# All columns of w_down as split products, a one-operation one-hot comparison, and table columns read by TensorE

## What is computed

```python
h = rmsnorm(x, g_pre_ffn[l]) * (1.0 + sc2) + sh2
gates = route(h, w_router, router_bias)        # 64 experts, 8 chosen for each token
g = jnp.einsum('sd,edf->sef', hs, w_gate)      # (1024 -> 256) for each expert
u = jnp.einsum('sd,edf->sef', hs, w_up)        # (1024 -> 256)
act = jax.nn.silu(g) * u * gs[:, :, None]
routed = jnp.einsum('sef,efd->sd', act, w_down)  # (256 -> 1024)
shared = (jax.nn.silu(h @ ws_gate) * (h @ ws_up)) @ ws_down
x = x + ga2 * rmsnorm(routed + shared, g_post_ffn[l])
```

## Time and profile before

| what | value |
|---|---|
| runs | 1063.95, 1064.50, 1066.36 us |
| the profiled execution | 1069.23 us |
| its span, first to last instruction | 1067.2 us |
| PE busy | 1020.3 us, 96% of the span |
| DVE busy | 872.1 us, 82% |
| ACT busy | 645.2 us, 60% |
| POOL busy | 295.4 us, 28% |
| L1366, the float32 half of down | 129.4 us busy in 272 records |
| L1372, the split half of down | 81.3 us busy in 136 records of the first form |
| L1845, `wdlo` | 82.7 us busy, 1216 ns each, x68 |
| L943, `wdhi` | 72.2 us busy, 1061 ns each, x68 |
| L1801, the one-hot comparisons | 61.2 us busy, 280 ns each, x284 |

### The profile page before, as it was taken

One profiled execution on the slowest core, in us unless ns is written; L12 is line 12 of the kernel. 1 busy time (PEld: TensorE's weight loads), 2 busy tenths in 40 slices (PEclk: granted clock), 3 DMA queues, 4 the chain that ended last, 5 costly groups with the idle time before them and its releaser, 6 DMA issues.

```text
span 1067.2 us, 15239 instructions
## 1 busy us (share of the span) xinstructions
PE 1020.3 (96%) x4652; PEld 742.9 (70%) x4652; DVE 872.1 (82%) x1416; ACT 645.2 (60%) x743; POOL 295.4 (28%) x224
## 2 busy tenths in 40 slices
PE   4999999899998999999999999999999999999976
PEld 0687776567754777777777777777777777777732
DVE  1669877734768899999999889999989999999867
ACT  5334135733343678777777767777767777777511
POOL 1242231630302433223323213323313323332200
PEclk9899999989999999999999999999999999999997
DMA  9667752212254799999999999999999999999993
GB/s 338 263 223 280 267 179 97 69 30 90 99 217 146 284 376 373 364 381 379 393 386 381 360 367 359 377 376 385 369 364 345 364 343 328 353 354 362 361 413 152
DMA packets 71080, 318.67 MB, mean 299 GB/s; under 512 B 17232, under 2 KB 17744, under 8 KB 44560
## 3 DMA queue, kind: packets, MB, share of 16 engines
q1 hardware_dynamic: 36816, 200.30, 49.7%
q10 hardware_dynamic: 11616, 72.66, 17.9%
q0 software_dynamic: 22624, 45.40, 11.4%
HBM read 317.25 MB, written 39.85 MB: 335 GB/s over the span
## 4 chain that ended last, share of the span: by engine, by line
PE 80%; DVE 9%; DMA 7%; ACT 2%; issue 1%; ACTq 0%; SPq 0%; POOL 0%; DVEq 0%; POOLq 0%
PE ps L1348 11%; PE ps L1350 11%; PE ps L1349 11%; PE ps L1366 10%; PE ps L1033 8%; PE ps L1372 8%; PE ps L1123 6%; DMA hg<-h_rows,idxg 3%; PE ps L1225 2%; DMA yr<-y_rows 2%; PE ps L1285 2%; PE ps L1049 2%; PE ps L1305 1%; PE ps L1207 1%; DVE acc L1504 1%
## 5 line engine op out<-in xcount | busy, mean ns | idle before, releaser
L1821 DVE TENSOR_TENSOR wlo<-raw,whi 128x2048 fp32r<-128x2048 f32 x136 | 305.2, 2285 | 0.0
L891 ACT ACTIVATE whi<-raw 128x2048 fp32r<-128x2048 f32 x136 | 261.4, 1923 | 0.0
L1348 PE MATMUL ps<-whi,hthi 128*128 128x512 f32 x544 | 223.9, 412 | 0.0
L1350 PE MATMUL ps<-whi,htlo 128*128 128x512 f32 x544 | 213.5, 393 | 0.0
L1349 PE MATMUL ps<-wlo,hthi 128*128 128x512 f32 x544 | 212.7, 391 | 0.0
L661 POOL DMA_INDIRECT y_rows<-ysb,idxs x68 | 69.1, 1016 | 447.8 <-DVE idxg L1816 387.2
L934 ACT ACTIVATE ysb<-ps 128x1024 f32<-128x1024 f32 x68 | 69.8, 1026 | 176.1 <-PE ps L1372 176.1
L653 POOL DMA_INDIRECT hg<-h_rows,idxg x70 | 135.9, 1942 | 71.9 <-DVE idxg L1816 51.6
L1366 PE MATMUL ps<-rawd,actt 128*128 128x512 f32 x272 | 129.4, 598 | 1.9 <-ACT actt L927 1.9
L1350 PEld LDWEIGHTS ps<-whi,htlo 128*128 128x128 f32 x544 | 102.1, 188 | 22.3
L1349 PEld LDWEIGHTS ps<-wlo,hthi 128*128 128x128 f32 x544 | 102.6, 189 | 17.7
(11 more groups left out here) (273 smaller groups left out, 1608.7 us busy)
## 6 DMA issues: line engine op xcount, KB each, us to landing
raw<-in_w_gate_dram SPq DMA_DIRECT2D x68, 1024.0 KB
raw<-in_w_up_dram SPq DMA_DIRECT2D x68, 1024.0 KB
rawd<-in_w_down_dram ACTq DMA_DIRECT2D x66, 1024.0 KB, 10.1
ada<-in_w_ada_dram SPq DMA_DIRECT2D x24, 1024.0 KB, 7.8
yr<-y_rows SPq DMA_DIRECT2D x6, 2048.0 KB, 19.1
wraw<-in_w_in_dram POOLq DMA_DIRECT2D x8, 1024.0 KB, 5.6
woraw<-in_w_out_dram SPq DMA_DIRECT2D x16, 256.0 KB, 2.7
yr<-y_rows SPq DMA_DIRECT2D x8, 512.0 KB, 10.1
```

The source lines that it names most:

```text
L891: A(whi[:, s, m_, :], raw[:, s, m_, :], ACT.Copy).then_inc(hi_ok, 1)
L1348: mm(out_, hthi[s][:, k, :], hi, start=(k == 0), stop=False)
L1350: ins = mm(out_, htlo[s][:, k, :], hi, start=False, stop=(k == KD - 1))
L1821: V.tensor_tensor(wlo[s][:, m_, :], raw[:, s, m_, :], whi[:, s, m_, :].bitcast(F32), ALU.subtract).then_inc(lo_dve, 1)
```

## The change

In `down`, the columns 512 to 1023 of `w_down` are also made of three split products, so PE has 12 fp32r products for each block. `down_high` and `down_low` work on both halves, in two operations each, and `wdhi[hf]` now belongs to a half, where it belonged to a slot. `down` waits for `actl` first, then for each half of `wdlo`. `actt` stays, as an operand of `actl`. `onehot` becomes one `tensor_tensor` of 4x128 elements, with both inputs broadcast, and without the copy to `vcur`; `indices` reads `vtab` at the block's number. PE therefore waits for `fill_ok` ahead of its loop, and its loop is cut in the same places as that of DVE. In the tail, `y_out(last, 0)` goes ahead of `down_high(last, 1)`.

```diff
--- before.py
+++ after.py
@@ -940,7 +940,8 @@
 
             def down_high(i, s):
                 ac.wait_ge(wd_in[s], i * 16 + 16)
-                A(wdhi[s][:, :, :], rawd[:, s, :, 0:DC], ACT.Copy).then_inc(wdhi_ok, 1)
+                for hf in range(2):
+                    A(wdhi[hf][:, :, :], rawd[:, s, :, hf * DC:(hf + 1) * DC], ACT.Copy).then_inc(wdhi_ok, 1)
 
             def step_act(i, s, late, e=None):
 
@@ -1012,8 +1013,8 @@
             down_high(last, 0)
             act_rows(last, 0)
             silu(last, 1)
+            y_out(last, 0)
             down_high(last, 1)
-            y_out(last, 0)
             act_rows(last, 1)
             y_out(last, 1)
 
@@ -1322,11 +1323,14 @@
                 ins.then_inc(count_mm, 1)
 
 
-            def indices(i, s):
+            def indices(i, s, shift=0):
 
                 pe.wait_ge(onehot_ok, num(i, s) + 1)
+                b = num(i, s) + shift
                 for t in range(TT):
-                    ins = mm(ps[:, 7 * BANK:7 * BANK + VC], s_onehot[:, t, :], vcur[:, t, :],
+                    src = vtab[:, t, b, :] if isinstance(b, int) else \
+                        vtab[:, t, bass.ds(b, 1), :].rearrange("p b v -> p (b v)")
+                    ins = mm(ps[:, 7 * BANK:7 * BANK + VC], s_onehot[:, t, :], src,
                              start=(t == 0), stop=(t == TT - 1))
                 ins.then_inc(idx_mm, 1)
 
@@ -1358,23 +1362,21 @@
                 ins.then_inc(at_tr, 1)
 
             def down(i, s):
-                pe.wait_ge(wd_in[s], i * 16 + 16)
-                pe.wait_ge(actt_ok, num(i, s) + 1)
+                pe.wait_ge(actl_ok, num(i, s) + 1)
                 if not (isinstance(i, int) and num(i, s) == 0):
                     pe.wait_ge(y_ok, num(i, s))
-                for k in range(KF):
-                    mm(bank(5), actt[:, k, :], rawd[:, s, k, DC:D], start=(k == 0), stop=(k == KF - 1))
-                pe.wait_ge(wdlo_ok, num(i, s) + 1)
-                pe.wait_ge(actl_ok, num(i, s) + 1)
-                for k in range(KF):
-                    for j, (a_, w) in enumerate(((acth, wdhi[s][:, k, :]), (acth, wdlo[:, s, k, 0:DC]),
-                                                 (actl, wdhi[s][:, k, :]))):
-                        ins = mm(bank(4), a_[:, k, :], w, start=(k == 0 and j == 0), stop=(k == KF - 1 and j == 2))
+                for hf in range(2):
+                    pe.wait_ge(wdlo_ok, num(i, s) * 2 + (hf + 1))
+                    for k in range(KF):
+                        hi, lo = wdhi[hf][:, k, :], wdlo[:, s, k, hf * DC:(hf + 1) * DC]
+                        mm(bank(4 + hf), acth[:, k, :], hi, start=(k == 0), stop=False)
+                        mm(bank(4 + hf), acth[:, k, :], lo, start=False, stop=False)
+                        ins = mm(bank(4 + hf), actl[:, k, :], hi, start=False, stop=(k == KF - 1))
                 ins.then_inc(dn_mm, 1)
 
-            def block_pe(i, s):
+            def block_pe(i, s, shift=0):
                 rows_in(*after(i, s, 1))
-                indices(*after(i, s, 3))
+                indices(*after(i, s, 3), shift)
                 gate_up(i, s, 0, 3)
                 acts_tr(*after(i, s, -1))
                 gate_up(i, s, 3, KD)
@@ -1426,14 +1428,16 @@
             mm(ps[:, OV + 128:OV + 128 + OVER], ones[0:E, :], jm[:, :], start=True, stop=True).then_inc(over_mm, 1)
             pe.wait_ge(over_ok, 1)
             block_pe(0, 1)
-            with pe.Fori(1, E // 2) as i:
+            pe.wait_ge(fill_ok, 1)
+            with pe.Fori(1, MID // 2 - 2) as i:
                 for s in range(SLOTS):
                     block_pe(i, s)
+            for b in range(MID - 4, MID):
+                block_pe(b // 2, b % 2, LASTE if b + 3 >= MID else 0)
             m = pe.value_load(npair[0:1, 0:1], min_val=0, max_val=OVER // 2)
-            with pe.If(m > 0):
-                with pe.Fori(E // 2, m + E // 2) as i:
-                    for s in range(SLOTS):
-                        block_pe(i, s)
+            with pe.Fori(MID // 2, m + E // 2) as i:
+                for s in range(SLOTS):
+                    block_pe(i, s, LASTE)
             acts_tr(m + (E // 2 - 1), 1)
             down(m + (E // 2 - 1), 1)
 
@@ -1793,13 +1797,9 @@
             def onehot(i, s, shift=0):
 
                 b = num(i, s) + shift
-                src = vtab[:, :, b, :] if isinstance(b, int) else \
-                    vtab[:, :, bass.ds(b, 1), :].rearrange("p t b v -> p t (b v)")
-                V.tensor_copy(vcur[:, :, :], src)
-                for t in range(TT):
-                    pcol = posb[:, t, b:b + 1] if isinstance(b, int) else posb[:, t, bass.ds(b, 1)]
-                    ins = V.tensor_scalar(s_onehot[:, t, :], iotab[:, :], pcol, None, ALU.is_equal)
-                ins.then_inc(onehot_ok, 1)
+                pcol = posb[:, :, b:b + 1] if isinstance(b, int) else posb[:, :, bass.ds(b, 1)]
+                V.tensor_tensor(s_onehot[:, :, :], iotab[:, :].unsqueeze(1).to_broadcast([P, TT, P]),
+                                pcol.to_broadcast([P, TT, P]), ALU.is_equal).then_inc(onehot_ok, 1)
 
             def tables(i, s):
                 b = num(i, s)
@@ -1841,9 +1841,11 @@
                 V.tensor_copy(idxs[s][:, :], col(destr, num(i, s))).then_inc(idxs_ok, 1)
 
             def down_low(i, s):
-                v.wait_ge(wdhi_ok, num(i, s) + 1)
-                V.tensor_tensor(wdlo[:, s, :, 0:DC], rawd[:, s, :, 0:DC], wdhi[s][:, :, :].bitcast(F32), ALU.subtract)\
-                 .then_inc(wdlo_ok, 1)
+                for hf in range(2):
+                    cols = slice(hf * DC, (hf + 1) * DC)
+                    v.wait_ge(wdhi_ok, num(i, s) * 2 + (hf + 1))
+                    V.tensor_tensor(wdlo[:, s, :, cols], rawd[:, s, :, cols], wdhi[hf][:, :, :].bitcast(F32),
+                                    ALU.subtract).then_inc(wdlo_ok, 1)
 
             def act_low(i, s):
                 v.wait_ge(acth_ok, num(i, s) + 1)
```

## The result

The changed kernel took 1075.7 us in the median of 10 runs (1071.1 to 1082.2), the kernel before 1066.4 us in 10 runs beside it: a ratio of 1.0092, with a 95% interval from 1.0076 to 1.0109. The two medians lie 9.3 us apart. The forecast was 1079 us: slower, by 14.6 us. The profiled execution took 1073.1 us, with a span of 1071.0 us at a mean granted clock of 0.983.

What follows compares the result with a forecast made beforehand. The prediction took PE to bound the kernel at 9.92 us a block; afterwards DVE and the loop through ACT would. Blocks +9.0, start +2.6 and tail +3.0 us gave +14.6 us, 1079 us, range 1069 to 1093 us.

Steps and rivals of the forecast that it cites:

- PE alone: Down on PE: twelve split products take 2.80 us instead of 3.12, making PE's own list 9.60 us a block.
- the signs: Trace signs that would show the forecast right, among them PE busy near 9.5 us of a 10.0 to 10.1 us block.
- its added wait: PE ahead of the first gate-up product: idle for about 0.45 us in each block.
- The bound of 0.7 us for the address: Upper bound on PE's sequencer cost for reading `vtab` at a computed place: 0.17 us at each of four products.
- rival 1: PE keeps the pace at its 9.60 us a block: -16 us, 1048 us; chance of being faster than before 0.11.
- DVE alone: DVE's work a block: second `wdlo` +1.13 us, one-hot -0.42 us, from 9.36 to 10.07 us.
- The gain ascribed to the one-hot operation: On DVE, one 0.60 us comparison replaces the copy and four comparisons of 1.02 us, saving 0.42 us a block.
- The loop through ACT: Wait loop over two blocks, PE to ACT to DVE to PE: 20.01 us, 10.0 us a block, against 9.69 today.
- The pace: Steady blocks: the larger of DVE's 10.07 and the loop's 10.0, taken as 10.06 us; +9.0 us over 64 distances.
- Start: Ahead of block 2, PE waits for `fill_ok` from POOL: +2.6 us, with bounds 1.1 and 3.5.
- Tail: After the last gate-up, the last down is 3.6 us later; +3 us taken, with bounds 0 and 5.
- The third rival: One-hot comparison on DVE no cheaper than what it replaces: 1107 us, or 1092 at half that loss; chance 0.08 for both.

Runs made afterwards that it cites:

- no_hi2_lo2: Changed kernel without the second `wdhi` on ACT and the second `wdlo` on DVE, all twelve products kept: 1062.9 us, 0.9951 times the kernel before.
- act_order: Changed kernel with ACT's `whi` of the first half moved behind the rows `actt` and `acth`: 1071.6 us, 1.0046 times the kernel before.
- split_only: Kernel before with only the second half of `w_down` split, old copy and four comparisons kept, no `fill_ok` wait: 1076.9 us, 1.0101.
- no_lo2: Changed kernel without the second `wdlo` on DVE; second `wdhi` and all twelve products stay: 1074.9 us, 1.0081 times the kernel before.
- fill_late: Changed kernel with PE's wait for `fill_ok` moved behind block 5: 1073.5 us, 1.0076 times the kernel before.
- after_again: The changed kernel once more, unmodified, for a second profile: 1073.3 us, 1.0077 times the kernel before.
- onehot_only: Kernel before with only the single comparison, `vtab` read by PE and the `fill_ok` wait; second half stays float32: 1066.2 us, 0.9990.

## Why the prediction was right

**PE alone: right.** 2.75 us for the twelve products against 2.80 us forecast, and 9.58 us for a block once nothing else is late (no_hi2_lo2). The address computation cost nothing. But the 0.32 us could not have been had in full: at 9.6 us a block the gathered rows come late, and the mean stays at 9.82 us. The prediction did not price that. PE's busy time is 9.70 us in the window and not near 9.5 as the signs had it. By distances its added wait is 1.30 - 0.98 = 0.32 us and 1.44 - 0.98 = 0.46 us in two blocks in a row, against 0.45 forecast. (The bound of 0.7 us for the address took 0.17 us as the smallest DVE operation; the rows have 0.16.) The late rows made rival 1 (1048 us) harder to reach than its chance said.

**DVE alone: 0.17 us too large, and on the wrong side of 9.92.** Forecast 10.07 us of work, "more than today's pace of 9.92". Measured 9.88 us in the step without a wait, and 9.91 us in the median where little else limits (act_order). So DVE's list alone would have cost nothing; this step of the prediction fails. The second `wdlo` and the one-hot operation cost what was worked out, (705.66 - 703.39) / 2 = 1.13 us and 0.60 us. What was off is the remainder of the old step, the 0.17 us that the prediction itself named as perhaps hidden behind a wait: where nothing is waited for, the reduce follows `idxs` at 701.67 - 701.62 = 0.05 us instead of 0.17 us, and `htlo` follows the reduce at 0.58 us instead of 0.64. The gain ascribed to the one-hot operation was off by more, 0.42 against 0.13 us a block (split_only). The row of 1.02 us held 0.29 us of `actl`'s wait for `acth`, a wait that the prediction itself uses in the loop through ACT ("`actl` starts 0.03 us later"). The sum didn't notice, since it took the whole 1.02 us out again: DVE's work before was 9.88 - 1.13 + 0.13 = 8.88 us, not 9.36, and rose by 1.00 us, not 0.71.

**The loop through ACT: right, and it is the bound, with DVE 0.1 us under it.** Forecast 10.0 us a block. no_lo2 isolates it at 10.02 us, and act_order, which shortens it, has a median block of 9.91 us. In the changed kernel DVE's steps alternate, 9.88 and 10.08 us, which is 19.96 us for two blocks against the 20.01 us summed up. The chain of waits between two gate-ups of the changed kernel runs as the list in the prediction did from the end of down on PE through ACT to `acth`. Behind that the profile's chain goes on through ACT's second `whi` and its silu to the second `wlo`, and not through `actl` and the first; that `actl` waits for `acth` is shown by the rows at 715.91 and 716.33 above:

```profile
649.76 0.25 PE ps L1374
650.11 0.08 ACT ysb L934
...
651.03 0.91 ACT hthi L923
...
652.89 0.90 ACT wdhi L944
653.84 1.92 ACT whi L891
...
656.02 0.27 ACT acth L928
656.29 0.91 ACT whi L891
...
657.98 0.40 ACT sg L919
...
658.87 2.29 DVE wlo L1821
661.21 0.50 PE ps L1352
```

**The pace: 9.99 us, not 10.06.** With DVE's work under the loop's 10.0 us, the larger of the two is 10.0. So the blocks cost +4.7 us over 63 distances, not +9.0 over 64. This term was mis-sized by 4.3 us, and the tail, below, by 3.3 us.

**Start: right, a little short.** Forecast +2.6 us (1.1 to 3.5), measured +3.2 (2.7 to 3.7), and undone by fill_late. The wait was 2.36 us: POOL's last copy ended 1.14 us behind the time at which PE wanted to begin, as read from before, the second `wdlo` added 0.83 us and not 1.1, and from POOL's last copy to PE's first transpose it took another 359.13 - 358.74 = 0.39 us. The rest is PE's clock, at its lower level (1.2 GHz, 0.51 granted) for some 3 us after the wait, which the prediction left out: the transposes took 1.92 us instead of 1.03.

**Tail: the wait was right, its cost was wrong.** The last down began 1025.99 - 1010.99 = 15.0 us behind the last block's first gate-up product, against 1017.19 - 1005.96 = 11.2 us before: 3.8 us later, and 3.6 were forecast. But the end of the span did not move (-0.3 us), where I had put +3. The reads and additions of the rank rows hid it. Only the last eight reads wait for the last down. They were issued 1040.17 - 1010.99 = 29.2 us behind that gate-up product, against 1030.95 - 1005.96 = 25.0 us before. DVE had the twelve additions of other rank rows (L1928, L1926 before) to do first in both kernels, and came to the rows of these reads after 1047.84 - 1010.99 = 36.9 and 1042.72 - 1005.96 = 36.8 us; and the reads landed in 7.7 us in the median instead of 10.1. At L1946 DVE waits 1.33 us, 0.21 in after_again, and 1.11 before:

```profile
1030.94 5.00 DVE L1928 TENSOR_TENSOR yr<-yr,yr 128x1024 f32<-128x1024 f32 x4 [3.99 <-DMA yr<-y_rows]
...
1051.69 1.23 DVE L1946 TENSOR_TENSOR yr<-yr,yr 128x1024 f32<-128x1024 f32 x1 [1.33 <-DMA yr<-y_rows]
```

Part of it may be PE's clock: before, PE waited 4.21 us for rank rows at 1040.19 us and then ran at 0.57 from 1040 to 1048; afterwards it ran at 1.00 from 1046 to 1050. How much of the 3.8 us each of these gave back is not shown: it was only read from the traces, and no run separates them.

Sum by what was measured: +4.7 + 3.2 - 0.3 = +7.6 us against +14.6 forecast. The direction rested on two bounds above 9.92 us. The loop through ACT stands and gives it; DVE's own list does not. The number came nearer than the terms did: 1079 lies 3.3 us above the 1075.7 measured, but the runs of the kernel before beside it had 1066.4 and not 1064.5 us, so the loss forecast, 14.6 us, was 5.3 us more than the 9.3 measured. That part is luck. The third rival (a one-hot operation no cheaper) was answered by its 0.60 us, and its price was too high: split_only keeps the old operations and takes 1076.9 us, not 1107. The range, which was stretched to 1093 us for its sake, was wider than it had to be.

## What to carry to other kernels

A change that moves work from PE to two other engines has to be summed along each loop that joins them, over as many blocks as its buffers allow: here the loop over two blocks gave the pace (10.0 us a block), DVE's own list lay 0.1 us under it, and so, by an estimate, did the loop over a single block. Taking work from one engine gives nothing while the loop passes by it (no_lo2: 1.13 us less for DVE, and the same pace). The cost of small operations is best read in a step where the engine never waits; where it waits, their distances are upper bounds (1.02 us against 0.73), and a wait can hide without a bracket: compare the start of an operation with the end of what it needs on the other engine (713.05 against 713.02). Before paying for a faster engine, ask what bounds it next: here PE without its other limits came to 9.58 us in the median and 9.82 us in the mean, since gathered rows landed late.

## What the runs showed of the hardware

- POOL's small copies stretch to the length of a two-input DVE operation that runs beside them: 2.33 and 2.27 us at L688 and L691 under `wlo` of 2.29 us, 1.19 us at L691 under a `wdlo` of 1.22 us, and 0.19 to 0.20 us at L691 otherwise. The Trainium skill, in "SBUF — State Buffer", section "SBUF: two separate sides", says that the port pair shared by the two is an exclusive lock held for the whole instruction; the trace agrees.
- After 2.36 us of idle time PE's granted clock fell to 0.51. After 1.33 us (onehot_only) the transposes kept their 1.09 us. The length of the wait alone does not settle it: after 1.93 us (before, at 1017.19) it was 0.56 from 1017 to 1019, and after 2.47 us (onehot_only, at 1016.03) it was 1.00 from 1016 to 1018.
- One comparison of 4x128 elements with both inputs broadcast takes 0.60 us of DVE's queue, and the copy of 24 elements with four comparisons of 128 takes 0.73 us (split_only).
- The common first 334 us vary by up to 5.7 us between profiles of kernels that are alike there.
